# Weight tiles stored in memory as the chip holds them: one run of 16 KB per partition instead of eight of 2 KB

## The chip, the core and the metric

The kernel runs on one core of a Trainium2 chip. TensorE (PE) multiplies matrices, VectorE (DVE) and ScalarE (ACT) do elementwise work and reductions, GpSimd (POOL) and SyncE (SP) here mostly issue transfers, and sixteen DMA engines, shared by all queues, carry the data between the chip's memory and the on-chip buffer of 128 partitions. The metric is the device time of one execution in microseconds (us), median of several runs.

## What is computed

Two transformer-like blocks in float32 over 256 tokens of width 1024, cut to what matters here:

```python
# first block
h = rms_norm(x, attn_norm_g)
q, k, v, qi, ki, wi, glu_in, gates = split(h @ w_in)
y_att  = dsa_attention(...) @ w_att_out        # top-64 keys of each query
y_conv = conformer_conv(glu_in, ...) @ w_conv_out
x = x + (g0 * y_att + g1 * y_conv) @ w_out
h2 = rms_norm(x, ffn_norm_g)
x = x + peer(h2, w_peer_q, sub_keys, peer_u, peer_v)   # 128 expert rows per token, gathered
x = x + sigmoid(rms_norm(x) @ w_ple_gate) * (p @ w_ple_proj)
# second block
mod = silu(c) @ ada_w + ada_b                  # six modulation vectors, also for the context
ctx states = scans of mixer_block(modulate(rms_norm(ctx)))
x = x + g1 * mixer_block(modulate(rms_norm(x)), ctx states) @ w_out
x = x + g2 * (silu(dwconv(h @ up_gate)) * (h @ up_value)) @ w_down
return rms_norm(x) * final_g
```

## The kernel before

All dense weights come in tiles, in one order fixed by `weight_tiles`: 54 of them, most 1024 rows by 512 columns (2048 KB), held on the chip as 128 partitions by 8 chunks of 512 numbers. Two slots of a ring (`weights`) take them in turn. `sp_weights` issues their loads on SP's queue (L482): tile i as soon as the PE work on tile i-2 is done (`tile_done`). In memory the weights are plain matrices, so that a partition's share of a tile is 8 runs of 2 KB; a tile `up` is two loads with runs of 1 KB, `kiwi` two with runs of some 270 B, `down` one with runs of 4 KB. SP's queue also carries x, the constants, `lora_up` and `ctx` (`sp_ctx`, ahead of the tile ctx_lora) and the output. `pe_tile` makes PE wait for a tile's landing; the matmuls of tiles are at L502, L512, L755, L760, L752, L1269, L2157 and L2454.

Other queues share the DMA engines. POOL first loads small tables (`rel_bias`, `onehot`; PE's first step, L791, needs them), then the modulation weights `in_ada_wT`: 48 loads of 512 KB in runs of 4 KB into four slots (L1119), each issued when DVE has used the load four before it. DVE uses one with each L1135 (from the 17th load on), and these steps are woven by hand between DVE's others: three before each of the products with conv_out and att_out (L1067, L1072, L1075), ten behind L1075, then L1087 (x plus the first half of mix_out), eight more, and L1091 (x plus the second half), on which the next norm and the expert queries (peer_q tiles) depend. The queries lead to DVE's selection, and the first selected quarter lets POOL start the gather: 256 indirect loads of 128 expert rows of 8 KB (L1475) into a ring of eight, used by DVE (L1490), ACT and PE (L1521). The second block's context work runs beside the gather. After the gather come the second block's projections, scans and feed-forward part.

Of the kernel before, what the change touches and what calls it, by code (L numbers as in the profile page):

```python
# [25 lines left out]
P = 128  # L26
# [3 lines left out]
DC = D // P  # L30
# [4 lines left out]
CC = CONV_CH // P  # L35
# [9 lines left out]
DFF = ((8 * D // 3 + 127) // 128) * 128  # L45
FC = DFF // P
# [14 lines left out]
WSLOTS = 2  # L61
# [19 lines left out]
def const_columns():  # L81

    widths = dict(ident=P, eps=1, gn_eps=1, flip=P, lower=CH, upper=CH, lower_eq=CH, upper_eq=CH, lower_neg=CH, upper_neg=CH, head_mean=P, head_mean2=2, conv_mean=P,
                  ident2=HD, hide=TB * T, reset=RC * T, iota=NCAND, ident_q=QP, quad=QUADS)
    at, out = 0, {}
    for name, n in widths.items():
        out[name] = (at, n)
        at += n
    return out, at  # L90
# [48 lines left out]
    return (np.arange(REL_BUCKETS)[:, None] == bucket[None]).astype(np.float32)  # L139

def weight_tiles(dram):

    order = []

    def tile(name, *parts, width=512):
        order.append((name, width, parts))

    def part(w, k0, kc, c0, n, at=0):  # L150
        return (w[k0 * P:(k0 + kc) * P, c0:c0 + n].rearrange("(k p) n -> p k n", p=P), kc, at, n)

    w = dram["w_in"]
    tile("glu_g", part(w, 0, DC, GLU0 + 512, 512))
    tile("glu_a", part(w, 0, DC, GLU0, 512))
    for name, c in (("q", Q0), ("k", K0), ("v", V0), ("qi", QI0)):
        tile(name, part(w, 0, DC, c, 512))
    tile("kiwi", part(w, 0, DC, KI0, 64), part(w, 0, DC, KI0, 72, 64), width=136)
    for i in range(4):
        tile(f"gate{i}", part(w, 0, DC, GATE0 + 512 * i, 512))  # L160
    for i in range(2):
        tile(f"conv_out{i}", part(dram["w_conv_out"], 0, CC, 512 * i, 512))
    for i in range(2):
        tile(f"att_out{i}", part(dram["w_att_out"], 0, CC, 512 * i, 512))
    for i in range(2):
        tile(f"mix_out{i}", part(dram["w_out"], 0, DC, 512 * i, 512))
    for i in range(4):
        tile(f"peer_q{i}", part(dram["w_peer_q"], 0, DC, 512 * i, 512))

    w = dram["w_in_2"]  # L170
    tile("ctx_k", part(w, 0, DC, K20, 512))
    tile("ctx_v", part(w, 0, DC, V20, 512))
    tile("ctx_lora", part(w, 0, DC, LORA0, 128), width=128)
    for i in range(2):
        tile(f"ple_proj{i}", part(dram["w_ple_proj"], 0, 2, 512 * i, 512))
    for i in range(2):
        tile(f"ple_gate{i}", part(dram["w_ple_gate"], 0, DC, 512 * i, 512))
    tile("x_k", part(w, 0, DC, K20, 512))
    tile("x_lora", part(w, 0, DC, LORA0, 256), width=256)
    for name, c in (("x_v", V20), ("x_r", R0), ("x_cc", CC0), ("x_cx", CX0), ("x_cb", CB0)):  # L180
        tile(name, part(w, 0, DC, c, 512))
    for i in range(2):
        tile(f"rw_out{i}", part(dram["w_out_2"], 0, DC, 512 * i, 512))
    for i in range(FC // 2):
        tile(f"up{i}", part(dram["ffn_w_up"], 0, DC, 256 * i, 256),
             part(dram["ffn_w_up"], 0, DC, DFF + 256 * i, 256, 256))
    for i in range(0, FC, 4):
        tile(f"down{i // 4}", part(dram["ffn_w_down"], i, min(4, FC - i), 0, 1024), width=1024)
    return order

def build(nc, dram, out_dram):
    SC, n_small = small_columns()
    KC, n_const = const_columns()
    tiles = weight_tiles(dram)
    tile_at = {name: i for i, (name, _, _) in enumerate(tiles)}

    with ExitStack() as ctx:
        sems = {}

        def S(name):
            if name not in sems:
                sems[name] = ctx.enter_context(nc.semaphore(name))
            return sems[name]
# [4 lines left out]
        def sb(name, shape, dt=F32):  # L209
            return whole(ctx.enter_context(nc.sbuf_tensor(name, shape, dt)), shape)  # L210
# [22 lines left out]
        ring = sb("weights", [P, WSLOTS, 4096])  # L233
# [225 lines left out]
        n_parts = [0, 0]  # L459
        landed_at = []  # L460
        for i, (_, _, parts) in enumerate(tiles):
            n_parts[i % WSLOTS] += len(parts)
            landed_at.append(16 * n_parts[i % WSLOTS])

        def sp_weights(sp):
            for i, (name, width, parts) in enumerate(tiles):
                if name == "rw_out0":
                    sv_ = Solve(sp, True)
                    for who in ("pe", "act", "dve"):
                        sv_.wait(who, 3, sv_.events[who][-1])  # L470
                if name == "ctx_lora":
                    sp_ctx(sp)
                if name == "ple_proj1":
                    sp_last_tokens(sp)
                if name == "ple_gate0":
                    sp.wait_ge(S("cdone"), 1)
                    sp.wait_ge(S("dots_ok"), TB * GROUPS)
                if i >= WSLOTS:
                    sp.wait_ge(S("tile_done"), i - WSLOTS + 1)
                for view, kc, at, n in parts:  # L480
                    dst = ring[:, i % WSLOTS, 0:kc * width].rearrange("p (k n) -> p k n", n=width)
                    sp.dma_start(dst[:, :, at:at + n], view).then_inc(S(f"landed{i % WSLOTS}"), 16)  # L482
                if i == 0:
                    sp.dma_start(const[:, CONST_HEAD:], dram["const"][:, CONST_HEAD:]).then_inc(S("const_rest"), 16)

        def pe_tile(pe, name, buffer=True):

            i = tile_at[name]
            _, width, parts = tiles[i]
            pe.wait_ge(S(f"landed{i % WSLOTS}"), landed_at[i])  # L490
            if buffer and i >= 2:
                pe.wait_ge(S(f"freed{i % 2}"), i // 2)
            kc = parts[0][1]
            return ring[:, i % WSLOTS, 0:kc * width].rearrange("p (k n) -> p k n", n=width), G[i % 2]

        def pe_features(pe, name, act, n_chunks=4):

            w, out = pe_tile(pe, name)
            kc = w.shape[1]
            for c in range(n_chunks):  # L500
                for k in range(kc):
                    mm = nc.tensor.matmul(out[:, c * T:(c + 1) * T], w[:, k, c * P:(c + 1) * P], act[:, k, :],  # L502
                                          start=(k == 0), stop=(k == kc - 1))
            mm.then_inc(S("tile_done"), 1)

        def pe_tokens(pe, name, act):

            w, out = pe_tile(pe, name)
            kc = w.shape[1]
            for b in range(TB):  # L510
                for k in range(kc):
                    mm = nc.tensor.matmul(out[:, b * 512:(b + 1) * 512], act[:, k, b * P:(b + 1) * P], w[:, k, :],  # L512
                                          start=(k == 0), stop=(k == kc - 1))
                if b == 0 and name in HALF_TILES:
                    mm.then_inc(S("half_done"), 1)
            mm.then_inc(S("tile_done"), 1)
# [689 lines left out]
        def sp_last_tokens(sp):  # L1206
            sp.wait_ge(S("normed_out"), 16)
            sp.dma_start(quad_last, normed_rows[P:2 * P]).then_inc(S("last_tokens"), 16)
# [441 lines left out]
        def sp_ctx(sp):  # L1650
            wait_freed(sp, "mix_out1")
            act_load(sp, "lora", loraup, dram["lora_up"].rearrange("d p n -> p d n"))
            sp.wait_ge(S("sc_pe"), QUARTERS * TB)
            act_load(sp, "ctx", ctok, dram["ctx"].rearrange("(b p) d -> p b d", p=P))
# [1068 lines left out]
        @block.sync  # L2723
        def _(sp):
            sp_start(sp)
            sp_weights(sp)
            sp_end(sp)
# [85 lines left out]
```

## Time and profile before

| | |
|---|---|
| median of 3 runs | 1560.54 us (1558.47 to 1561.19) |
| span of the profiled execution | 1554.9 us |
| PE busy | 1212.9 us (78%) |
| DVE busy | 926.5 us (60%) |
| ACT / POOL busy | 431.5 us / 347.1 us |
| DMA | 409.73 MB in 109720 packets, mean 264 GB/s |
| of it SP's queue (q1) | 106.48 MB in 63552 packets, 19.2% of 16 engines |
| of it POOL's queue (q0) | 297.35 MB in 44576 packets, 46.5% |

A busy share is a mean over stages that have different limits; the stages have to be read one by one. The profiled execution's own time is its span of 1554.9 us; the runs' median lies 5.6 us above it.

### The profile page before, as it was taken

What the parts mean: (1) busy time and instruction counts of PE and PEld (TensorE: products, weight loads), DVE (VectorE), ACT (ScalarE), POOL (GpSimd) and SP (SyncE); (2) the same over time, 40 slices, a digit from 0 to 9 for tenths busy, and PEclk for the clock granted to TensorE, in tenths of its full rate; (3) what the DMA queues carried; (4) which work ended last, traced back from release to release, by engine and by line L of the source; (5) the groups of instructions that cost most, each with busy time, mean ns of one, the idle gap of its engine ahead of it and who ended that gap; (6) DMA issues with size and microseconds to landing.
All of it is one profiled execution on the core that took longest, in us unless ns stands there. A gap on an engine that the chain in (4) does not pass through costs nothing.

```text
span 1554.9 us, 26679 instructions
## 1 busy us (share of the span) xinstructions
PE 1212.9 (78%) x11282; PEld 834.9 (54%) x11282; DVE 926.5 (60%) x2067; ACT 431.5 (28%) x1094; POOL 347.1 (22%) x315
## 2 busy tenths in 40 slices
PE   7989898894385533457856775799987888999998
PEld 6467784772153100125524452468877774888843
DVE  2887666657797988785677655321455343455512
ACT  2111420132432422543364332423243211110100
POOL 1000012034354555454455544000000000000000
PEclk9997999996597855569878996899999999999999
DMA  9551459699999999999999999624300023344432
GB/s 381 195 191 66 144 205 390 238 383 419 414 410 420 420 422 421 421 414 419 416 421 420 420 418 418 240 82 163 109 9 3 4 111 108 122 163 161 137 140 104
DMA packets 109720, 409.73 MB, mean 264 GB/s; under 512 B 8456, under 2 KB 33552, under 8 KB 76448
## 3 DMA queue, kind: packets, MB, share of 16 engines
q0 software_dynamic: 44576, 297.35, 46.5%
q1 hardware_dynamic: 63552, 106.48, 19.2%
q10 hardware_dynamic: 1472, 4.20, 1.0%
q8 instruction: 88, 1.44, 0.4%
q14 instruction: 32, 0.26, 0.0%
HBM read 405.89 MB, written 2.11 MB: 262 GB/s over the span
## 4 chain that ended last, share of the span: by engine, by line
PE 58%; DMA 22%; DVE 10%; ACT 4%; issue 3%; POOL 2%; another core or an unknown queue 0%; POOLq 0%; DVEq 0%; ACTq 0%; SPq 0%
PE psum L502 20%; DMA arena<-in_experts,arena 17%; PE psum L1942 8%; PE psum L2454 5%; PE psum L512 4%; DVE arena L1490 4%; PE psum L1521 3%; DMA arena<-in_lora_up 2%; PE psum L755 2%; PE psum L1269 2%; POOL arena L1475 2%; PE psum L2244 2%; PE psum L760 2%; DMA arena<-in_ada_wT 2%; PE psum L741 2%
## 5 line engine op out<-in xcount | busy, mean ns | idle before, releaser
L1475 POOL DMA_INDIRECT arena<-in_experts,arena x256 | 317.1, 1239 | 383.2 <-PE psum L1521 299.8
L1521 PE MATMUL psum<-arena 128*32 128x512 f32 x1024 | 185.4, 805 | 238.2 <-ACT arena L1506 231.6
L502 PE MATMUL psum<-actT,weights 128*128 128x256 f32 x1312 | 287.3, 381 | 0.0
L502 PEld LDWEIGHTS psum<-actT,weights 128*128 128x128 f32 x1312 | 250.3, 191 | 35.7 <-issue 1.5
L1521 PEld LDWEIGHTS psum<-arena 128*32 128x32 f32 x1024 | 22.7, 121 | 329.5 <-ACT arena L1506 307.3
L1490 DVE CUSTOM_DVE_ANT_0 arena<-arena 128x1024 f32<-128x1024 f32 x96 | 116.7, 1224 | 50.9 <-DMA arena<-in_experts,arena 50.1
L1490 DVE CUSTOM_DVE_ANT_0 arena<-weights,arena 128x1024 f32<-128x1024 f32 x96 | 116.6, 1223 | 37.1 <-DMA arena<-in_experts,arena 35.1
L1496 ACT ACTIVATE arena<-arena 128x2 f32<-128x2 f32 x128 | 26.1, 204 | 364.3 <-DVE arena L1490 350.4
L1942 PE MATMUL psum<-arena 64*64 64x64 f32 (+1 forms) x2816 | 89.7, 231 | 17.4 <-DVE arena L2059 7.1
L1942 PEld LDWEIGHTS psum<-arena 64*64 64x64 f32 x2816 | 84.1, 142 | 26.0 <-issue 14.6
L1490 DVE CUSTOM_DVE_ANT_0 arena<-normed,arena 128x1024 f32<-128x1024 f32 x64 | 77.2, 1225 | 22.1 <-DMA arena<-in_experts,arena 20.3
L1119 POOL DMA_DIRECT2D arena<-in_ada_wT x48 | 25.5, 531 | 229.7 <-DVE mod L1135 229.7
L2454 PE MATMUL psum<-weights,arena 128*128 128x512 f32 x176 | 75.7, 592 | 0.0
L512 PE MATMUL psum<-weights,actT 128*128 128x512 f32 x160 | 69.2, 592 | 0.0
L1506 ACT ACTIVATE arena<-const,arena 128x32 f32<-128x32 f32 x256 | 66.3, 306 | 0.0
L1501 ACT ACTIVATE arena<-arena 128x1 f32<-128x1 f32 x256 | 61.5, 287 | 12.1 <-ACT arena L1496 0.4
L2528 DVE SCALAR_TENSOR_TENSOR arena<-arena,small 128x256 f32<-128x256 f32 x154 | 61.9, 478 | 0.0
L2454 PEld LDWEIGHTS psum<-weights,arena 128*128 128x128 f32 x176 | 33.4, 190 | 41.7 <-issue 41.6
L1942 PEld LDWEIGHTS psum<-actT,arena 64*64 64x64 f32 x1152 | 39.3, 134 | 21.4 <-ACT arena L2027 12.0
L512 PEld LDWEIGHTS psum<-weights,actT 128*128 128x128 f32 x160 | 30.4, 190 | 37.8 <-issue 37.8
L1942 PE MATMUL psum<-actT,arena 64*64 64x64 f32 x1152 | 45.5, 221 | 5.7 <-issue 4.3
L675 ACT ACTIVATE normed<-xres 128x512 f32<-128x512 f32 (+1 forms) x13 | 9.0, 692 | 146.4 <-DVE xres L2544 60.3
(390 smaller groups left out, 1897.0 us busy)
## 6 DMA issues: line engine op xcount, KB each, us to landing
weights<-in_w_in SPq DMA_DIRECT2D x18, 2048.0 KB
arena<-in_ada_wT POOLq DMA_DIRECT2D x48, 512.0 KB, 6.3
weights<-in_ffn_w_up SPq DMA_DIRECT2D x22, 1024.0 KB
weights<-in_ffn_w_down SPq DMA_DIRECT2D x5, 2048.0 KB
weights<-in_w_out SPq DMA_DIRECT2D x4, 2048.0 KB
weights<-in_w_peer_q SPq DMA_DIRECT2D x4, 2048.0 KB
arena<-in_experts,arena POOLq DMA_INDIRECT x256
weights<-in_w_ple_gate SPq DMA_DIRECT2D x2, 2048.0 KB
```

What stands on the lines that cost most here:

```text
L502: mm = nc.tensor.matmul(out[:, c * T:(c + 1) * T], w[:, k, c * P:(c + 1) * P], act[:, k, :], start=(k == 0), stop=(k == kc - 1))
L512: mm = nc.tensor.matmul(out[:, b * 512:(b + 1) * 512], act[:, k, b * P:(b + 1) * P], w[:, k, :], start=(k == 0), stop=(k == kc - 1))
L741: mm = nc.tensor.matmul(chunk_bank(c)[:, b * P:(b + 1) * P], xres[:, b, c * P:(c + 1) * P], norm_diag[:, b, :], start=True, stop=True)
L755: mm = nc.tensor.matmul(out[:, 2 * i * T:(2 * i + 1) * T], w[:, k, 2 * i * P:(2 * i + 1) * P], actT[:, k, :], start=(k == 0), stop=(k == D ...
L1475: nc.gpsimd.indirect_dma_start(out=rows[:, n % RING, :], out_offset=None, in_=dram["experts"], in_offset=bass.IndirectOffsetOnAxis(ap=eidx ...
L1490: ins = nc.vector.tensor_tensor_reduce(rows[:, pos, 0:D], quad_row(b, k % QUADS), rows[:, pos, 0:D], 1.0, 0.0, ALU.mult, ALU.add, dots[:, ...
L1501: nc.scalar.activation(acts[:, g, j:j + 1], gelu[:, g, j:j + 1], ACT.Copy, scale=gate[:, b, bass.ds(t * RING + (g * GROUP + j), 1)]).then_ ...
L1506: nc.scalar.activation(diag[:, pos, :], K("ident_q"), ACT.Copy, scale=acts[:, g, j:j + 1]).then_inc(S("diag_ok"), 1)
L1521: mm = nc.tensor.matmul(SUMS[sum_part(k, i), i, :], diag[:, pos, :], rows[:, pos, D + 512 * i:D + 512 * (i + 1)], start=first, stop=last, ...
L1942: mm = nc.tensor.matmul(dst[half[c], g, at + q * n:at + (q + 1) * n], left(g, c, q), right(g, c, q), start=True, stop=True)
L2454: return nc.tensor.matmul(aux[2 * b + n], ffT[:, f, b * P:(b + 1) * P], w[:, k, 512 * n:512 * (n + 1)], start=(f == 0), stop=(f == FC - 1))
L2528: st.run(nc.vector.scalar_tensor_tensor(dst, src, w, dst, ALU.mult, ALU.add))
```

## The change

Each weight tile is laid out beforehand as its own array of 128 rows, one row for each partition, in the order in which the chip holds it. A load is then one run for each partition: 16 KB for a full tile. `up` and `kiwi` become one load instead of two, and the counts that PE waits for follow (one landing for each tile). Tiles, order, slots, waits and arithmetic stay. Two tiles with the same contents (ctx_k and x_k, for one) share an array.

```diff
-    def part(w, k0, kc, c0, n, at=0):
-        return (w[k0 * P:(k0 + kc) * P, c0:c0 + n].rearrange("(k p) n -> p k n", p=P), kc, at, n)
+    def part(key, k0, kc, c0, n, at=0):
+        return key, k0, kc, c0, n, at
...
+def tile_sources():
+    first = {}
+    for name, _, parts in weight_tiles():
+        first.setdefault(parts, "tile_" + name)
+    return first
+
+def tile_arrays(arrays):
+    out = {}
+    for parts, name in tile_sources().items():
+        cuts = [arrays[key][k0 * P:(k0 + kc) * P, c0:c0 + n].reshape(kc, P, n) for key, k0, kc, c0, n, at in parts]
+        out[name] = np.ascontiguousarray(np.concatenate(cuts, axis=2).transpose(1, 0, 2)).reshape(P, -1)
+    return out
...
-            n_parts[i % WSLOTS] += len(parts)
+            n_parts[i % WSLOTS] += 1
...
-                for view, kc, at, n in parts:
-                    dst = ring[:, i % WSLOTS, 0:kc * width].rearrange("p (k n) -> p k n", n=width)
-                    sp.dma_start(dst[:, :, at:at + n], view).then_inc(S(f"landed{i % WSLOTS}"), 16)
+                kc = parts[0][2]
+                sp.dma_start(ring[:, i % WSLOTS, 0:kc * width], dram[sources[parts]]).then_inc(S(f"landed{i % WSLOTS}"), 16)
```

## Rows read from the trace of the kernel before

**Rows 1.** The page's second section: DMA busy tenths and rate in 40 slices.

```profile
DMA  9551459699999999999999999624300023344432
GB/s 381 195 191 66 144 205 390 238 383 419 414 410 420 420 422 421 421 414 419 416 421 420 420 418 418 240 82 163 109 9 3 4 111 108 122 163 161 137 140 104
```

**Rows 2.** Stretches: busy of PE, PEld, DVE, ACT, POOL (instructions); granted clock, DMA share, GB/s.

```profile
258.00:263.00 5.00, 5.00 (x14) 2.13 (x13) 3.95 (x7) 1.63 (x5) 1.27 (x3) 1.00 0.95 303
263.00:272.00 9.00, 8.74 (x21) 3.61 (x19) 4.93 (x8) 0.00 (x0) 1.92 (x4) 1.00 1.03 414
...
276.00:280.00 4.00, 1.72 (x8) 1.72 (x9) 2.46 (x8) 1.75 (x5) 0.53 (x1) 0.50 1.03 415
...
318.00:984.00 666.00, 408.51 (x4640) 216.53 (x4638) 491.21 (x1194) 253.42 (x793) 317.15 (x256) 0.76 1.01 418
...
420.00:440.00 20.00, 14.11 (x85) 8.10 (x85) 19.62 (x56) 6.41 (x23) 9.14 (x8) 0.83 0.97 393
...
1334.00:1472.00 138.00, 138.00 (x641) 121.49 (x640) 76.36 (x190) 16.87 (x41) 0.00 (x0) 1.00 0.45 153
```

**Rows 3.** POOL's waits, 300 to 985 us: us in total, times, longest.

```profile
POOL arena L1475 <- DVE arena L1444: 41.6, 1, 41.6
```

**Rows 4.** Timeline of DVE: start, us, operation [idle before, releaser].

```profile
240.00 1.23 DVE L1075 TENSOR_TENSOR arena<-arena 128x1024 f32<-128x1024 f32 x1
...
255.84 1.23 DVE L1135 CUSTOM_DVE_ANT_0 arena<-arena 128x1024 f32<-128x1024 f32 x1
257.11 1.23 DVE L1135 CUSTOM_DVE_ANT_0 arena<-arena 128x1024 f32<-128x1024 f32 x1
258.26 1.22 DVE L1087 TENSOR_TENSOR xres<-psum,xres 128x1024 f32<-128x1024 f32 x1
...
268.66 1.23 DVE L1135 CUSTOM_DVE_ANT_0 arena<-arena 128x1024 f32<-128x1024 f32 x1 [0.76 <-DMA arena<-in_ada_wT]
...
274.55 1.22 DVE L1135 CUSTOM_DVE_ANT_0 arena<-arena 128x1024 f32<-128x1024 f32 x1 [0.72 <-DMA arena<-in_ada_wT]
275.70 1.28 DVE L1091 TENSOR_TENSOR xres<-psum,xres 128x512 f32<-128x512 f32 x2
```

**Rows 5.** Timeline of PE around mix_out and at two norms.

```profile
242.34 2.44 PE L512 MATMUL psum<-weights,arena 128*128 128x512 f32 x4 [3.70 <-issue]
...
261.71 10.03 PE L512 MATMUL psum<-weights,arena 128*128 128x512 f32 x23
278.28 2.95 PE L741 MATMUL psum<-normed,xres 128*128 128x128 f32 x12 [6.54 <-DVE normed L722]
...
1316.62 1.83 PE L741 MATMUL psum<-normed,xres 128*128 128x128 f32 x12 [2.64 <-DVE normed L722]
```

**Rows 6.** Timeline of SP's queue: when a weight tile is issued.

```profile
231.14 0.37 SPq L482 DMA_DIRECT2D weights<-in_w_out  x1
238.67 0.37 SPq L482 DMA_DIRECT2D weights<-in_w_out  x1
258.04 0.37 SPq L482 DMA_DIRECT2D weights<-in_w_peer_q  x1
271.77 0.37 SPq L482 DMA_DIRECT2D weights<-in_w_peer_q  x1
...
356.53 0.37 SPq L482 DMA_DIRECT2D weights<-in_w_in  x1
```

**Rows 7.** The chain that ended last, in order of time: start, us, what.

```profile
356.95 32.78 DMA arena<-in_lora_up
...
389.81 11.80 DMA arena<-in_ctx
```

**Rows 8.** DMA issues: line, count, KB each, median us to landing.

```profile
xres<-in_x SPq DMA_DIRECT2D x1, 1024.0 KB, 5.1
...
bias_rows<-arena POOLq DMA_DIRECT2D x1, 12.0 KB, 4.8
```

**Rows 9.** The same chain at the start.

```profile
1.97 5.07 DMA arena<-in_onehot
```

More of the change, by code:

```diff
@@ L139, in bucket_onehot, with weight_tiles @@
     return (np.arange(REL_BUCKETS)[:, None] == bucket[None]).astype(np.float32)
-def weight_tiles(dram):
+def weight_tiles():
     order = []
@@ L148, in tile @@
         order.append((name, width, parts))
-    def part(w, k0, kc, c0, n, at=0):
-        return (w[k0 * P:(k0 + kc) * P, c0:c0 + n].rearrange("(k p) n -> p k n", p=P), kc, at, n)
-    w = dram["w_in"]
+    def part(key, k0, kc, c0, n, at=0):
+        return key, k0, kc, c0, n, at
+    w = "w_in"
     tile("glu_g", part(w, 0, DC, GLU0 + 512, 512))
@@ L161, in weight_tiles @@
     for i in range(2):
-        tile(f"conv_out{i}", part(dram["w_conv_out"], 0, CC, 512 * i, 512))
+        tile(f"conv_out{i}", part("w_conv_out", 0, CC, 512 * i, 512))
     for i in range(2):
-        tile(f"att_out{i}", part(dram["w_att_out"], 0, CC, 512 * i, 512))
+        tile(f"att_out{i}", part("w_att_out", 0, CC, 512 * i, 512))
     for i in range(2):
-        tile(f"mix_out{i}", part(dram["w_out"], 0, DC, 512 * i, 512))
+        tile(f"mix_out{i}", part("w_out", 0, DC, 512 * i, 512))
     for i in range(4):
-        tile(f"peer_q{i}", part(dram["w_peer_q"], 0, DC, 512 * i, 512))
-    w = dram["w_in_2"]
+        tile(f"peer_q{i}", part("w_peer_q", 0, DC, 512 * i, 512))
+    w = "w_in_2"
     tile("ctx_k", part(w, 0, DC, K20, 512))
@@ L174, in weight_tiles @@
     for i in range(2):
-        tile(f"ple_proj{i}", part(dram["w_ple_proj"], 0, 2, 512 * i, 512))
+        tile(f"ple_proj{i}", part("w_ple_proj", 0, 2, 512 * i, 512))
     for i in range(2):
-        tile(f"ple_gate{i}", part(dram["w_ple_gate"], 0, DC, 512 * i, 512))
+        tile(f"ple_gate{i}", part("w_ple_gate", 0, DC, 512 * i, 512))
     tile("x_k", part(w, 0, DC, K20, 512))
@@ L182, in weight_tiles @@
     for i in range(2):
-        tile(f"rw_out{i}", part(dram["w_out_2"], 0, DC, 512 * i, 512))
+        tile(f"rw_out{i}", part("w_out_2", 0, DC, 512 * i, 512))
     for i in range(FC // 2):
-        tile(f"up{i}", part(dram["ffn_w_up"], 0, DC, 256 * i, 256),
-             part(dram["ffn_w_up"], 0, DC, DFF + 256 * i, 256, 256))
+        tile(f"up{i}", part("ffn_w_up", 0, DC, 256 * i, 256),
+             part("ffn_w_up", 0, DC, DFF + 256 * i, 256, 256))
     for i in range(0, FC, 4):
-        tile(f"down{i // 4}", part(dram["ffn_w_down"], i, min(4, FC - i), 0, 1024), width=1024)
+        tile(f"down{i // 4}", part("ffn_w_down", i, min(4, FC - i), 0, 1024), width=1024)
     return order
+def tile_sources():
[9 more added lines that the diff above has]
+    return out
 def build(nc, dram, out_dram):
@@ L194, in build @@
     KC, n_const = const_columns()
-    tiles = weight_tiles(dram)
+    tiles, sources = weight_tiles(), tile_sources()
     tile_at = {name: i for i, (name, _, _) in enumerate(tiles)}
@@ L492, in pe_tile @@
                 pe.wait_ge(S(f"freed{i % 2}"), i // 2)
-            kc = parts[0][1]
+            kc = parts[0][2]
             return ring[:, i % WSLOTS, 0:kc * width].rearrange("p (k n) -> p k n", n=width), G[i % 2]
@@ L2801 @@
         "final_g": a["final_g_2"],
-        "w_in": a["w_in"][0], "w_conv_out": a["w_conv_out"][0], "w_att_out": a["w_att_out"][0],
-        "w_out": a["w_out"][0], "w_peer_q": a["w_peer_q"][0], "ada_wT": np.ascontiguousarray(a["ada_w_2"][0].T),
-        "w_in_2": a["w_in_2"][0], "w_ple_gate": a["w_ple_gate"][0], "w_ple_proj": a["w_ple_proj"][0],
-        "w_out_2": a["w_out_2"][0], "ffn_w_up": a["ffn_w_up_2"][0], "ffn_w_down": a["ffn_w_down_2"][0],
+        "ada_wT": np.ascontiguousarray(a["ada_w_2"][0].T),
+        **tile_arrays({
+            "w_in": a["w_in"][0], "w_conv_out": a["w_conv_out"][0], "w_att_out": a["w_att_out"][0],
+            "w_out": a["w_out"][0], "w_peer_q": a["w_peer_q"][0], "w_in_2": a["w_in_2"][0],
+            "w_ple_gate": a["w_ple_gate"][0], "w_ple_proj": a["w_ple_proj"][0], "w_out_2": a["w_out_2"][0],
+            "ffn_w_up": a["ffn_w_up_2"][0], "ffn_w_down": a["ffn_w_down_2"][0],
+        }),
     }
```

## The prediction

> **What bounds the kernel now.** I read the page's forty slices first: of 38.9 us each: the DMA engines are full in the first, in the seventh (233 to 272 us) and from the ninth to the twenty-fifth (the gather); elsewhere they have room [rows 1]. That splits the weight tiles, which all travel on SP's queue, into three kinds. (a) Tiles loaded beside a busy PE. From 1334 to 1472 us PE is busy 138.00 of 138.00 us while DMA stands at 0.45 [rows 2]; there a faster load is worth nothing, because each 2048 KB tile (2.10 MB) has 13.8 us of PE work in front of it. The same goes for the slices around 1014 to 1130 us, at 82 to 163 GB/s [rows 1]. (b) Tiles loaded during the gather of expert rows, which moves 418 GB/s over 666 us [rows 2]; its end is set by bytes, and the change moves the same bytes. The gather's first instruction waits 41.6 us for DVE's first selection [rows 3], so whatever delays that selection delays everything behind it. (c) Tiles loaded between 224 and 283 us, beside the stream of modulation weights (`in_ada_wT`, 48 loads of 512 KB, four slots, POOL's queue). Here is the place that counts: in the timeline of DVE each L1135 waits for a load, and L1091, which adds the last half of mix_out, stands behind the last of them and starts at 275.70 [rows 4]. PE had finished mix_out1 at 271.74 and sits idle until 278.28 [rows 5]. So about 4 us of the path are DMA, not PE.
>
> **Who gets the DMA.** lora_up (0.52 MB) was issued behind ctx_v (2.10 MB, issued at 356.53) on SP's queue [rows 6] and took 32.78 us [rows 7]: 2.62 MB in 32.8 us is 80 GB/s, 0.19 of 418. Both have 2 KB runs, the expert rows beside them 8 KB: 2/(2+8) is 0.20. The ctx load behind them (1.05 MB, 4 KB runs) took 11.80 us [rows 7]; without 2.6 us for start and finish (the xres load: 5.1 us for 1.05 MB, of which 2.5 is bytes at 414 GB/s [rows 8]) that is 114 GB/s, 0.27, against 4/12 = 0.33. And while peer_q0 loads in 2 KB runs, the last L1135 come 1.96 us apart (268.66 to 274.55, three steps) [rows 4]: 0.524 MB / 1.96 us is 267 of 414 GB/s [rows 2], 0.65, against 4/(4+2) = 0.67. So each DMA engine seems to give each queue one run in turn, and a queue's share goes by the length of its runs. With 16 KB runs the weights would take 16/20 = 0.80 beside ada_wT (332 GB/s, and 83 are left) and 16/24 = 0.67 beside the experts. The bytes stay; who is served first changes.
>
> The Trainium skill, "DMA: Bandwidth & Descriptors", section "Queues, rings and completion order", says that a DMA engine goes round the queues packet by packet, and a packet there holds some 9 to 17 descriptors. The trace agrees on the turns, but its 0.19 fits turns of one run. If a turn held so many runs of either queue, the shares would be the same.
>
> **Term A, the stretch from 231 to 276 us.** mix_out0 is issued at 231.14 [rows 6]; landing at 231.14 + 2.6 + 2.10/0.332 = 240.1. PE starts on it at 242.34 [rows 5], though DVE's last product ended at 241.23 [rows 4]: with the tile there, PE starts at 241.3, 1.0 us earlier. mix_out1 (issued 238.67) lands by 247.6, peer_q0 (issued 257) by 266. In each of these three windows of 6.3 us ada_wT gets 0.52 MB, one load where it now gets three. It loses four loads before L1087 and makes them up alone: alone, L1135 come 1.27 us apart (255.84 to 257.11 [rows 4]). Ten L1135 stand between L1075 and L1087. Two find their loads there (241.3 and 242.5), the third waits until about 247.0, seven more at 1.26 end at 257.1; L1087 starts at 257.1 instead of 258.26. Eight more follow: two at 258.4 and 259.6, the third inside the peer_q0 load at about 263.5, five more from 265.4 at 1.27 apart; the last ends at 271.8, against 275.77. PE, 1.0 us earlier, ends mix_out1 at 270.7, so L1091 starts at 271.8: A = -4.0. From 258 to 263 the trace moves only 303 GB/s where 414 follow [rows 2], a loss of 1.3 us; with 16 KB runs waiting I expect that hole closed, and -4.0 contains this. Bounds: -4.5 (PE's end decides) and +3 (below, second rival). I take -3.5, near the hand schedule, since the four slots may not restart without a gap.
>
> **Term B, PE's clock after that wait.** After 6.54 us idle the twelve L741 records take 2.95 us; in the later stage with the same code, after 2.64 us idle, 1.83 [rows 5]. The granted clock was 0.50 from 276 to 280 us [rows 2], the 1.2 GHz level. With a gap of 2.6 to 3 us some of the 1.1 us goes: B = -0.5, bounds -1.1 and 0.
>
> **Term C, the gather.** It starts earlier by A + B and lasts as long, since it is bytes. peer_q3 lands about when the gather begins. ctx_v needs about 2.6 + 2.10/0.28 = 10 us instead of most of 32.8, lora_up and ctx follow some 17 us earlier, and DVE, which now waits for ctx, no longer crowds the work behind it: from 420 to 440 us DVE is busy 19.62 of 20 and the DMA rate falls to 393 [rows 2], a loss of 25 GB/s for 20 us, 1.2 us. I take half: C = -0.6, bounds -1.2 and +0.5 (if the bursts of 67% open such a hole elsewhere).
>
> **Term D, the start.** PE's first step waits for onehot, 48 KB on POOL's queue, issued at 1.97, 5.07 us [rows 9]. Its last runs meet glu_g on SP's queue, and with 16 KB runs a turn is eight times longer: 16 KB at 414/16 GB/s is 0.63 us instead of 0.08. The nearest row is the bias_rows store, 4.8 us [rows 8], which ran beside the 9.6 KB runs of const: no slower. So 0 by that row, at most two turns, 1.3 us; D = +0.4.
>
> **Term E, fewer instructions.** kiwi and eleven up tiles need one DMA instead of two: 12 issues of 0.37 us on SP's queue [rows 6], all where SP waits for PE. Cost nothing, gain nothing; if SP were late the tile would still have its 13.8 us. PE waits on the same tiles; no wait is added, and nothing new stands behind one.
>
> **Sum.** -3.5 - 0.5 - 0.6 + 0.4 = -4.2 us on the profiled 1554.9 us of span. The median of the runs, 1560.54, lies 5.6 us above that span, which I carry over: 1556.3.
>
> **Rivals.** First (the forecast, 0.53): 1556.3, its own range 1554 to 1558.5. Second, slower (0.19): the last L1135 must have its load before peer_q1, issued when PE ends mix_out1 at 270.7, brings its first bytes about 1.5 us later, at 272.2. My schedule has that load landed at 270.5, 1.7 us ahead. If stalls of the four slots eat this margin, the load meets a queue that takes 0.80, and what is left of 0.52 MB goes at 83 GB/s, up to 6.3 us instead of 1.3: L1091 at 277 to 279 instead of 275.7. A is then about +2, B 0, C -0.6, D +0.4: 1562.3. For it speaks that ada_wT has only four slots; against it that the loads make 1.27 us each when alone. No load here has them; at half the rate the 7.6 MB of weights inside the gather (peer_q3, ctx_k, ctx_v, ctx_lora, ple_proj) would cost 18 us: 1578.
>
> By the section "Specifications" of the same page of the Trainium skill, runs of 512 B or more already go at line rate. By that rule the length of a run gains nothing in itself, which is the third rival's time, 1560.5, with its chance; the trace agrees as far as 2 KB runs beside 4 KB ones move 414 GB/s.
>
> **How the numbers follow.** About 0.2% (3.1 us) is what a measurement here can tell from no change. The forecast's own spread puts 0.43 below 1557.4 and 0.10 above it; with the third rival within 0.2% is 0.33; second and fourth give slower 0.24. The range 1554 to 1563.5 leaves out some 0.07 below, the fourth rival and the upper part of the second.
>
> **What would show it.** Right: lora_up lands after some 15 us instead of 32.78; PE starts mix_out0 near 241.3; L1135 shows two long waits (some 3 to 4 us) in place of seven short ones; L1091 near 272; the first gather near 314.5; and the rest shifted as one piece. Wrong: lora_up unchanged (third rival), a wait of over 3 us right before L1091 (second), tiles of 2.10 MB that take over 8 us when alone (fourth), onehot landing after 8 us (D too small).

## The result

The changed kernel takes 1565.22 us (median of 6 runs, 1563.46 to 1567.41); the kernel before, run beside it, 1559.84 us (6 runs, 1557.52 to 1561.59). The ratio is 1.0034, 95% interval 1.0023 to 1.0046: slower by some 5.4 us, where 4.2 us faster was forecast. The same kernel measured again gave 1.0043 (e11, below). The profiled span is 1561.4 us against 1554.9.

First the changes in traffic that were meant. From the page of the changed kernel, the DMA part of the slices and the count of packets:

```profile
GB/s 386 193 189 67 137 222 376 207 349 420 420 422 421 415 422 422 420 419 417 419 420 419 420 418 413 254 81 162 108 9 3 4 111 108 122 162 160 135 143 101
DMA packets 55767, 409.72 MB, mean 262 GB/s; under 512 B 6216, under 2 KB 6736, under 8 KB 16096
```

Half the packets (before: 109720), the same bytes. In the seventh and the eighth slice (233 to 311 us) the rate is lower than before: 376 and 207 instead of 390 and 238 [rows 1].

Now the place that counts. The timeline of DVE in the changed kernel (start, us, operation, [idle before, releaser]); all line numbers have grown by 16, so that L1151 is the former L1135, L1103 the former L1087 and L1107 the former L1091:

```profile
245.39 1.23 DVE L1151 CUSTOM_DVE_ANT_0 arena<-arena 128x1024 f32<-128x1024 f32 x1 [1.89 <-DMA arena<-in_ada_wT]
249.10 1.23 DVE L1151 CUSTOM_DVE_ANT_0 arena<-arena 128x1024 f32<-128x1024 f32 x1 [2.48 <-DMA arena<-in_ada_wT]
...
259.62 1.22 DVE L1103 TENSOR_TENSOR xres<-psum,xres 128x1024 f32<-128x1024 f32 x1
264.07 1.23 DVE L1151 CUSTOM_DVE_ANT_0 arena<-arena 128x1024 f32<-128x1024 f32 x1 [3.23 <-DMA arena<-in_ada_wT]
...
271.99 1.23 DVE L1151 CUSTOM_DVE_ANT_0 arena<-arena 128x1024 f32<-128x1024 f32 x1 [0.41 <-DMA arena<-in_ada_wT]
279.60 1.23 DVE L1151 CUSTOM_DVE_ANT_0 arena<-arena 128x1024 f32<-128x1024 f32 x1 [6.37 <-DMA arena<-in_ada_wT]
280.75 1.22 DVE L1151 CUSTOM_DVE_ANT_0 arena<-arena 128x1024 f32<-128x1024 f32 x1
281.89 1.29 DVE L1107 TENSOR_TENSOR xres<-psum,xres 128x512 f32<-128x512 f32 x2
```

One wait of 6.37 us stands two steps ahead of L1107, which starts at 281.89 instead of 275.70 [rows 4]: +6.2 us. DVE's waits for these loads from 231 to 285 us (us in total, times, longest), in the kernel before and below it in the kernel after, differ by as much:

```profile
DVE arena L1135 <- DMA arena<-in_ada_wT: 11.2, 12, 2.2
```

```profile
DVE arena L1151 <- DMA arena<-in_ada_wT: 17.5, 9, 6.4
```

The load that DVE waits for is the last link of the DMA kind on the chain that ended last in this stretch (start, us, what); the first line is one from the stretch's beginning, for comparison:

```profile
242.65 7.71 DMA arena<-in_ada_wT
...
268.74 10.83 DMA arena<-in_ada_wT
```

The two weight tiles beside it, from the timeline of SP's queue (start of the first, time from there to the end of the second, count):

```profile
255.18 14.06 SPq L498 DMA_DIRECT2D weights<-in_tile_peer_q  x2
```

peer_q0 is issued at 255.18 and peer_q1 at about 268.9, that is 0.2 us after the slow load of 512 KB; before, they went at 258.04 and 271.77 [rows 6]. Why they go earlier is on the timeline of PE:

```profile
241.14 27.73 PE L528 MATMUL psum<-weights,arena 128*128 128x512 f32 x64 [2.65 <-DVE arena L1091]
284.47 0.80 PE L757 MATMUL psum<-normed,xres 128*128 128x128 f32 x2 [15.60 <-DVE normed L738]
```

mix_out starts 1.2 us earlier (242.34 before) and its 64 matmuls take 27.73 us instead of 29.40, so PE is done at 268.87 instead of 271.74 [rows 5], and then idles 15.60 us instead of 6.54. Everything behind is moved as one piece, as POOL's first gather and its wait show:

```profile
324.54 1.01 POOL L1491 DMA_INDIRECT arena<-in_experts,arena  x1 [41.74 <-DVE arena L1460]
```

It stands 6.28 us later than before (318.26), its wait for the selection as long as it was (41.6 [rows 3]).

Cut into stages by the first instructions of each, the profiles read (us; "to L1107" is from mix_out0's issue to the second add; "to gather" from there to the first gather; "gather" up to the issue of ple_gate0; "rest" to the end of the span):

| kernel | span | to mix_out0 | to L1107 | to gather | gather | rest |
|---|---|---|---|---|---|---|
| before | 1554.9 | 231.14 | 44.56 | 42.56 | 670.28 | 566.4 |
| after | 1561.4 | 230.92 | 50.97 | 42.65 | 669.60 | 567.3 |

Of +6.5 us, +6.4 lie in one stage of 45 us, -0.7 in the gather, +0.9 in the rest, where PE's clock stood on another level at one norm (below, term B).

### The profile page after: what moved, and what is told of

Read it like the earlier page. It is cut to its first block, busy times and chain, and to the rows that moved or that the text cites. A ratio compares the mean times of both kernels' runs of the same rounds, so it can differ in the third digit from the quotient of the medians.

```text
span 1561.4 us, 26667 instructions
## 1 busy us (share of the span) xinstructions
PE 1208.4 (77%) x11282; PEld 828.9 (53%) x11282; DVE 927.6 (59%) x2067; ACT 430.3 (28%) x1094; POOL 350.1 (22%) x315
## 3 DMA queue, kind: packets, MB, share of 16 engines
q0 software_dynamic: 44576, 297.35, 46.5%
## 4 chain that ended last, share of the span: by engine, by line
PE 54%; DMA 27%; DVE 9%; ACT 4%; issue 3%; POOL 2%; POOLq 0%; DVEq 0%; ACTq 0%
DMA arena<-in_experts,arena 23%; PE psum L518 19%; PE psum L1958 5%; PE psum L2470 5%; PE psum L528 4%; DVE arena L1506 3%; PE psum L1537 3%; POOL arena L1491 2%; DMA arena<-in_ada_wT 2%; PE psum L771 2%; PE psum L2260 2%; PE psum L776 2%; PE psum L1285 2%; PE psum L757 2%; PE psum L768 1%
## 5 line engine op out<-in xcount | busy, mean ns | idle before, releaser
L1537 PE MATMUL psum<-arena 128*32 128x512 f32 x1024 | 189.4, 820 | 249.2 <-ACT arena L1522 249.0
L1958 PE MATMUL psum<-arena 64*64 64x64 f32 (+1 forms) x2816 | 82.4, 226 | 15.4 <-DVE arena L2075 7.1
L1958 PEld LDWEIGHTS psum<-arena 64*64 64x64 f32 x2816 | 78.5, 139 | 23.6 <-issue 12.2
L1135 POOL DMA_DIRECT2D arena<-in_ada_wT x48 | 25.3, 528 | 236.1 <-DVE mod L1151 236.1
L2470 PEld LDWEIGHTS psum<-weights,arena 128*128 128x128 f32 x176 | 33.4, 190 | 41.7 <-issue 41.6
L757 PE MATMUL psum<-normed,xres 128*128 128x128 f32 x160 | 29.4, 329 | 26.5 <-DVE normed L738 21.5
```

Source lines behind the costliest of these rows:

```text
L757: mm = nc.tensor.matmul(chunk_bank(c)[:, b * P:(b + 1) * P], xres[:, b, c * P:(c + 1) * P], norm_diag[:, b, :], start=True, stop=True)
L1537: mm = nc.tensor.matmul(SUMS[sum_part(k, i), i, :], diag[:, pos, :], rows[:, pos, D + 512 * i:D + 512 * (i + 1)], start=first, stop=last, ...
L1958: mm = nc.tensor.matmul(dst[half[c], g, at + q * n:at + (q + 1) * n], left(g, c, q), right(g, c, q), start=True, stop=True)
L2470: return nc.tensor.matmul(aux[2 * b + n], ffT[:, f, b * P:(b + 1) * P], w[:, k, 512 * n:512 * (n + 1)], start=(f == 0), stop=(f == FC - 1))
```

## The experiments

The theory after the result: a DMA engine gives the queues turns of equally many runs, so that weight tiles in 16 KB runs take most of the traffic beside the 4 KB runs of `in_ada_wT`; the modulation loads between mix_out0 and L1107 come late, and one of the last meets peer_q1. The main rival: tiles in an order of their own are slower to load or cost PE time, wherever they are. All ratios are to the kernel before, run beside each batch, with 95% intervals.

**Length of the runs alone (e1, e12, e8).** The tiles stay arrays of their own, but in blocks, so that a partition's share comes in eight runs of 2 KB (e1) or four of 4 KB (e12, and e8, the same kernel run once for its profile):

```diff
-                sp.dma_start(ring[:, i % WSLOTS, 0:kc * width], dram[sources[parts]]).then_inc(...)
+                r = runs_of(sources[parts][5:], kc)        # e1: kc; e8, e12: max(kc // 2, 1)
+                dst = ring[:, i % WSLOTS, 0:kc * width].rearrange("p (r m) -> p r m", r=r)
+                sp.dma_start(dst, dram[sources[parts]].rearrange("(r p) m -> p r m", p=P)).then_inc(...)
```

> Each tile still lies in memory by itself, as in the changed kernel, but cut into eight blocks of 128 rows, so that a partition gets eight runs of 2 KB as in the kernel before; one load for each tile. Theory (turns: a DMA engine takes one run of each queue in turn, and 16 KB runs of the peer_q tiles crowd out the modulation weights): as the kernel before, ratio 0.998 to 1.002, lora_up lands after 31 to 34 us, the add of mix_out's second half starts at 275 to 276.5 us. Rival (place: where the tile lies in memory or its regular step is what costs): as the changed kernel, ratio 1.003, lora_up as in the changed kernel (17 us), the add near 282 us.

> All tiles cut into blocks so that a partition gets four runs of 4 KB (two rows of 2 KB joined). Only one look, for the share of a queue by its run length. Theory (turns): beside 8 KB expert rows the weights get 4/12; lora_up, behind ctx_v, lands after 22 to 26 us (32.8 at 2 KB, 17.3 at 16 KB). Rival (share by queue, not by run): 31 us or more, or 18 or less as with 16 KB.

> e8 (four runs of 4 KB for each partition), now timed: the weights and the modulation weights, whose runs are 4 KB too, share evenly. Theory: no load waits over 3 us before the add, 44 to 46 us after mix_out0 is issued; the gather keeps about half of its 0.6 us; ratio 0.998 to 1.001. Rival (tile order costs by itself, as in e1): ratio 1.002 to 1.005.

e1: 1564.63 us, 1.0040 (1.0024 to 1.0056). e12: 1560.52 us, 1.0015 (0.9999 to 1.0031). e8: one run of 1556.17 us. e12's ratio lies between what was expected of the theory (up to 1.001) and of the rival (from 1.002). The stage to L1107 is 44.8 us in e1, 44.8 in e12 and 45.1 in e8: with short runs the long wait is gone. The load of lora_up behind ctx_v, which measures a queue's share beside the gather, follows the run. From the DMA issues (last column: median us to landing) of e8, and below it of the kernel after:

```profile
arena<-in_lora_up SPq DMA_DIRECT2D x1, 512.0 KB, 24.1
```

```profile
arena<-in_lora_up SPq DMA_DIRECT2D x1, 512.0 KB, 17.2
```

32.8 us with 2 KB [rows 7] (34.6 in e15), 24.1 with 4 KB, 17.2 with 16 KB. With the prediction's shares (ctx_v's run over itself plus 8 KB, 2/10 for lora_up behind it, 418 GB/s) and its 2.6 us for start and finish, an estimate gives some 34, 24 and 16. So a queue's share follows the length of its runs, and "shares don't follow the run" (third rival) is out. The Trainium skill, "DMA: Bandwidth & Descriptors", section "Queues, rings and completion order", has a DMA engine go round its queues by packets of some 9 to 17 descriptors. The three times don't speak against that: turns of equally many runs give the same shares as turns of one run, so these times can't tell one from the other.

But e1's total is not that of the kernel before, which was expected. Its profile has +1.5 us ahead of mix_out0 (no evidence, since this stage lies between 230.6 and 232.8 us in all profiles) and +3.3 from the fourth norm to x_cc, where PE waits 0.47 us for x_v and then runs 64 matmuls in 15.77 us instead of 14.06. That cost is taken up again with e16.

**Which of the peer_q tiles (e2, e3, e5).** e2 is e1 with peer_q1 alone in 16 KB runs (`r = 1 if name == "peer_q1" else kc`), e3 the changed kernel with peer_q0 and peer_q1 in blocks of 2 KB runs (`r = kc if name in ("peer_q0", "peer_q1") else 1`). e5 is the kernel before with peer_q1 alone as an array in 16 KB runs; all others come from their matrices:

```diff
+                if name in LONG:                            # LONG = ("peer_q1",)
+                    sp.dma_start(ring[:, i % WSLOTS, 0:kc * width], dram[tile_key(name)]).then_inc(...)
+                else:
                     for key, k0, kc, c0, n, at in parts:
```

> All tiles as in e1 (eight runs of 2 KB) but peer_q1, which has one run of 16 KB. Theory (turns): PE ends mix_out1 at about 271.7 and peer_q1 goes out; the last load of modulation weights that the add needs is then half landed and gets a fifth of the engines, so one wait of 3 to 6 us (now 0.7) stands before the add, which starts at 278 to 281 us; ratio 1.0015 to 1.0035. Rival (it takes all the tiles, or peer_q0's load is what costs): ratio within 0.999 to 1.001, the add at 275 to 276.5 us.

> All tiles with one run for each partition, but peer_q0 and peer_q1 with eight of 2 KB. Theory (turns): the mix_out tiles still land early, PE ends mix_out1 at 269 us as in the changed kernel, the long wait before the add is gone, the add starts at 272 to 276 us, the gather keeps its 0.6 us: ratio 0.997 to 1.000. Rival (late landing of all tiles, or their place, is what costs): ratio 1.002 to 1.0035, the add after 279 us.

> The kernel before, every tile read from its matrix as it was, but peer_q1 alone laid out with one run of 16 KB for each partition (e1 has shown that 2 KB runs in the tile's own order are themselves slower, so that e2 had no clean base). Theory (turns): one wait of 3 to 7 us in front of the add of mix_out's second half instead of 0.7; the add starts 48 to 50.5 us after mix_out0 is issued (44.6 in the kernel before); ratio 1.002 to 1.004. Rival (the loss needs long runs in all tiles, or is in the later stages): 44 to 46 us, ratio 0.999 to 1.001.

e2: 1564.34 us, 1.0025 (1.0006 to 1.0045), stage to L1107 50.2 us, with one wait of 4.86 us before the last step: peer_q1's long runs bring a wait back into e1's profile. On the time e2 is no slower than e1 (1.0040), and its profile is of the slowest of its seven runs (1569.35 us), so the wait's price is not shown by this pair. e3: 1560.18 us, 1.0014 (1.0000 to 1.0028), 45.7 us: without the two tiles' long runs the wait is gone, but the expected 0.997 to 1.000 was missed. e5: 1557.96 us, 0.9995 (0.9979 to 1.0011), 44.6 us: here the expected wait of 3 to 7 us did not come. Its timeline of DVE ends ahead of the add with

```profile
274.09 1.22 DVE L1155 CUSTOM_DVE_ANT_0 arena<-arena 128x1024 f32<-128x1024 f32 x1 [0.62 <-DMA arena<-in_ada_wT]
```

and PE in e5 ended mix_out1 only at 272.2 (242.81 + 29.40), so that peer_q1, issued at 272.24, found the last modulation load nearly landed. So peer_q1's long runs alone did no harm here, where they started behind these loads. That speaks for a race, which the changed kernel loses from both sides: PE is earlier and the loads are later. e2 fits in: its loads came in 2 KB runs as in e5, but PE's 64 matmuls took 27.70 us and not 29.40, so that peer_q1 went out 1.7 us sooner after mix_out's start.

**The four tiles of the stretch (e6, e14).** The changed kernel, but mix_out0, mix_out1, peer_q0 and peer_q1 come from their matrices in 2 KB runs (`LONG` = all names but these four); e14 is the same kernel once more.

> The changed kernel, but the four tiles that load beside the modulation weights (mix_out0, mix_out1, peer_q0, peer_q1) are read from their matrices in 2 KB runs as in the kernel before. Theory (turns): the whole loss is gone; the add starts 44 to 46 us after mix_out0 is issued, the gather lasts 0.6 us less; ratio 0.998 to 1.0005. Rival (part of the loss is in other tiles or later stages): ratio 1.002 or more.

> The kernel of e6_after_but_mix_peer once more, unchanged: the changed kernel with mix_out0, mix_out1, peer_q0 and peer_q1 read from their matrices in runs of 2 KB. If the whole loss lies in the stretch from mix_out0 to L1091: L1091 at 42.5 to 45 us after the issue of mix_out0 and the ratio to the kernel before 0.998 to 1.000, as at first (42.9 us, 0.9992). If the layout of the other tiles loses something elsewhere: above 1.001.

e6: 1556.66 us, 0.9992 (0.9977 to 1.0007); e14: 1558.88 us, 0.9995 (0.9982 to 1.0008). Stage to L1107 42.9 and 45.1 us. In e6 the last steps of DVE run without a wait:

```profile
270.80 1.22 DVE L1155 CUSTOM_DVE_ANT_0 arena<-arena 128x1024 f32<-128x1024 f32 x1 [0.81 <-DMA arena<-in_ada_wT]
271.95 1.22 DVE L1155 CUSTOM_DVE_ANT_0 arena<-arena 128x1024 f32<-128x1024 f32 x1
273.18 1.22 DVE L1155 CUSTOM_DVE_ANT_0 arena<-arena 128x1024 f32<-128x1024 f32 x1
274.33 1.28 DVE L1111 TENSOR_TENSOR xres<-psum,xres 128x512 f32<-128x512 f32 x2
```

So the loss goes with four tiles of 54, and the other fifty in 16 KB runs cost nothing that can be measured (the intervals end at 1.0007 and 1.0008), and gain nothing. That also answers the main rival for 16 KB runs; e4 and e10 below answer it from the other side, since there every tile keeps its order and runs and only the time of issue changes. A version that beats the kernel before by more than its interval was not found.

**peer_q1 alone undone (e9, e13).** The changed kernel with peer_q1 alone from its matrix; e13 is the same kernel again.

> The changed kernel with peer_q1 alone read from its matrix in 2 KB runs. e5 showed no loss from a 16 KB peer_q1 alone, since the last load of modulation weights had landed before its first bytes. Theory (a race: the early mix_out0 and the late modulation weights let peer_q1 come in front of the last two loads, and its 16 KB runs then keep them waiting): the 6 us wait shrinks to 1 to 2.5 us, the add starts 44.5 to 47 us after mix_out0 is issued, ratio to the kernel before 0.9985 to 1.0015. Rival (peer_q0's long runs are the loss, peer_q1 only shows it): 49 us or more, ratio 1.002 to 1.004.

> The kernel of e9_after_peer_q1_2k once more, unchanged: the changed kernel with peer_q1 alone read from its matrix in runs of 2 KB. In its first profile L1091 still came 49.5 us after the issue of mix_out0 (four single waits of 0.7 to 2.2 us in place of one of 6.4), yet its time was 0.35% below that of the changed kernel. If peer_q1's long runs alone make the loss: the ratio again 1.000 to 1.002, and L1091 mostly before 47 us. If the three other tiles do their part, as that profile says: L1091 again near 49.5 us and the ratio 1.001 to 1.003. If that timing was luck: 1.003 or more.

e9: 1560.99 us, 1.0008 (0.9996 to 1.0020); e13: 1563.63 us, 1.0026 (1.0012 to 1.0040). The stage to L1107 took 49.5 and 49.1 us, where 44.5 to 47 was expected. DVE in e13:

```profile
260.45 1.22 DVE L1107 TENSOR_TENSOR xres<-psum,xres 128x1024 f32<-128x1024 f32 x1
261.59 1.21 DVE L1155 CUSTOM_DVE_ANT_0 arena<-arena 128x1024 f32<-128x1024 f32 x1
267.65 1.23 DVE L1155 CUSTOM_DVE_ANT_0 arena<-arena 128x1024 f32<-128x1024 f32 x1 [4.84 <-DMA arena<-in_ada_wT]
...
278.06 1.22 DVE L1155 CUSTOM_DVE_ANT_0 arena<-arena 128x1024 f32<-128x1024 f32 x1 [2.83 <-DMA arena<-in_ada_wT]
280.06 1.23 DVE L1155 CUSTOM_DVE_ANT_0 arena<-arena 128x1024 f32<-128x1024 f32 x1 [0.76 <-DMA arena<-in_ada_wT]
281.21 1.28 DVE L1111 TENSOR_TENSOR xres<-psum,xres 128x512 f32<-128x512 f32 x2
```

The wait during peer_q1 is shorter (2.83 for 6.37), but the one during peer_q0 is there (4.84), and the loads behind it come that much later. My first reading, that peer_q1 alone makes the loss, was too narrow: by these profiles peer_q0's long runs make the loads late, and peer_q1's then add to it. How much of the loss is each tile's share these two timings leave open between 1.0008 and 1.0026.

**Holding the tiles back (e4, e10, e7).** SP waits until DVE has used so many modulation loads before it issues a peer_q tile. e4 is the changed kernel with both held, e10 with peer_q1 alone, e7 the kernel before with peer_q0 held until 42 and, as 16 KB runs, only the tiles loaded inside the gather (peer_q3, ctx_k, ctx_v, ctx_lora, ple_proj):

```diff
+                for held, used in (("peer_q0", 41), ("peer_q1", 44)):      # e10: peer_q1 alone
+                    if name == held:
+                        sp.wait_ge(S("ada_used"), used)
```

> The changed kernel, with two waits on SP's queue: peer_q0 goes out when 41 of the 48 loads of modulation weights are used, peer_q1 when 44 are (those that stand before the add). Theory (turns): with no other load beside them the last eight uses come about 1.3 us apart, the add starts at 268.5 to 272 us, PE may then wait up to 2 us for peer_q0; ratio 0.995 to 0.998. Rival (the loss is in the tiles themselves): ratio 1.001 to 1.004, and later peer_q tiles make it worse.

> The changed kernel with one wait on SP's queue: peer_q1 goes out when 44 loads of modulation weights are used, that is with the add. Theory (race): the last two loads come without a neighbour, 1.3 to 1.8 us apart, the add starts 44 to 46.5 us after mix_out0 is issued, peer_q1 still lands 10 us before PE needs it; ratio 0.998 to 1.001. Rival (peer_q0's long runs): 48 us or more, ratio 1.0015 or more.

> The kernel before with 16 KB runs only for tiles that load beside the gather (peer_q3, ctx_k, ctx_v, ctx_lora, ple_proj), and with a wait on SP's queue: peer_q0 goes out when 42 of 48 loads of modulation weights are used. Theory (turns): the eight uses behind the first add come about 1.3 us apart, the second add starts 40.5 to 42 us after mix_out0 is issued (PE's end of mix_out1 then decides), peer_q0 lands just in time (0 to 1 us of wait), the gather lasts 0.6 us less: ratio 0.9965 to 0.999. Rival (the modulation stream is bound by its four slots and its queue, not by sharing): 44 to 45 us, ratio 0.999 to 1.002.

e4: 1559.62 us, 1.0007 (0.9991 to 1.0023), stage to L1107 41.75 us, the next one 46.3. e10: 1560.1 us, 1.0005 (0.9989 to 1.0020), 47.5 us. e7: 1561.19 us, 1.0021 (1.0004 to 1.0038), 41.0 us, the next one 50.4. The gains expected of e4 and e7 (up to 0.998 and 0.999) did not come. With the tiles out of the way the second add comes 3 us earlier than before, which is what the change hoped for, but then PE waits for the tile that was held, 0.57 us in e4 and 5.02 in e7, and works behind it at a granted clock of 0.50 (e4, 280 to 286 us; 0.90 in the kernel before). PE in e7:

```profile
275.11 2.95 PE L763 MATMUL psum<-normed,xres 128*128 128x128 f32 x12 [2.95 <-DVE normed L744]
283.08 2.08 PE L777 MATMUL psum<-actT,weights 128*128 128x256 f32 x4 [5.02 <-DMA weights<-in_w_peer_q]
```

So these orders of issue got no 4 us out of the stretch: the loads of both queues are needed at its end, and who is served first decided who waits. A hold that ends earlier was not tried. e10 shows on the time what peer_q1's place is worth (1.0005 against 1.0043 in the same batch), by a way that leaves the run length alone. Its profile, of one of its slowest runs (1562.96 us), missed the expected 44 to 46.5 us: a wait of 5.58 us stands in it beside peer_q0's long runs.

**The changed kernel and the kernel before again (e11, e15).** No edits.

> The changed kernel as it is, once more beside the next three, so that they have it on the same chip. Expected: ratio 1.002 to 1.005, one wait of 5 to 7 us before the add of mix_out's second half, which starts 50 to 52 us after mix_out0 is issued.

> The kernel before, once more, for the spread of one kernel's stages between two profiles. If differences of 1 to 2 us between profiles in stages that no edit touches (from the start to mix_out0 230.6 to 232.8 us, from the fourth norm to x_cc 59.3 to 62.1, from there to the fifth norm 222.4 to 225.7) are the chip's own: such a stage of this profile differs from the first one (231.1, 60.9, 224.6) by 1 us or more while L1091 stays at 44 to 46 us after mix_out0. If they belong to the kernels: all within 0.5 us of the first profile. Ratio 0.998 to 1.002.

e11: 1564.8 us, 1.0043 (1.0023 to 1.0062), stage to L1107 50.9 us, with one wait of 7.39 us ahead of the last two steps: the wait stands in both profiles of the changed kernel. e15: 1558.54 us, 0.9995 (0.9983 to 1.0007), stage to L1107 44.7 us. But other stages, which no edit touches, differ between the two profiles of the kernel before: from the add to the gather 42.56 and 44.13, from the fourth norm to x_cc 60.91 and 59.45 us. Differences of 1 to 1.6 us there are no evidence for a kernel. The stage to L1107 varies too: in five profiles of kernels that read its four tiles alike, from the matrices (before, e15, e6, e14 and e16), it took 42.9 to 47.3 us. e10's 47.5 lies at the edge of that, the 50.9 and 51.0 of the changed kernel and the 49.1 to 50.2 of e13, e9 and e2 clearly outside.

**Where 2 KB runs in blocks lose (e16).** The kernel before with the block order of e1 from ctx_k on; the tiles up to peer_q3 come from their matrices.

> The kernel before, but the tiles from ctx_k on are arrays of their own in tile order, with eight runs of 2 KB for each partition, as in e1_runs2k; the tiles up to peer_q3 come from their matrices. e1 cost 0.4% without any long wait. If that cost is in the loads of the second block (x_v landing 0.5 us late, and a lower granted clock behind it): ratio 1.003 to 1.005, and PE waits some 0.5 us for x_v. If it is in the first 320 us: 0.999 to 1.001. A value between says both.

e16: 1561.33 us, 1.0023 (1.0008 to 1.0037), between the two answers. The 64 matmuls of x_v take 14.08 us and do not wait, so that e1's slow x_v was not the place. And the stage to L1107, where its edits do nothing, took 47.3 us in its profile, with PE's clock up in mix_out (27.70 us for the 64) and peer_q0 out at 256.2. So what e1 and e16 lose is not settled: the length of a run doesn't explain it, nor do the late tiles' loads by any wait that I found; where the arrays lie in memory was not tried.

**PE's clock at mix_out.** The 64 matmuls of mix_out take 27.70 to 27.73 us in six of the eighteen profiles (after, e11, e2, e6, e9, e16) and 29.20 to 30.27 in the other twelve. With 2.65 us of idle time ahead of them both occur: 27.73 in after, e11 and e9, and 29.20 to 29.27 in e3, e4, e10 and e13. With 3.48 us or more there are only long ones (before 3.70, e15 3.48, e5 4.54). The granted clock decides. Over the first 2 us of mix_out (columns as in [rows 2]), in the kernel after and below it in e13:

```profile
241.10:243.10 2.00, 1.96 (x5) 1.00 (x6) 1.98 (x3) 0.00 (x0) 0.45 (x1) 1.00 1.12 469
```

```profile
241.80:243.80 2.00, 2.00 (x3) 0.97 (x4) 2.00 (x3) 0.00 (x0) 0.51 (x1) 0.50 1.12 469
```

After the same 2.65 us idle it is 1.00 in one (2.4 GHz) and 0.50 in the other (1.2 GHz). That gives or takes 1.6 us of PE's end, and so of peer_q1's issue. Both profiles of the changed kernel have the upper level; what its wait would be at the lower one is not shown. The nearest pair is e9 and e13, with 49.5 us at the upper level and 49.1 at the lower.

## Why the prediction was wrong, point by point

**What bounds, and the shares: right.** The stretch from 231 to 276 us was the one that decided, and a queue's share followed its run: lora_up took 17.2 us, where some 15 was forecast, ctx_v's long runs ahead of it included.

**Term A: the step that failed.** It was to give -3.5 us and measured +6.2. The second rival had the mechanism (a late modulation load that meets peer_q1's long runs), the mark in the profile (a wait of over 3 us right before the add) and the size of the wait (up to 6.3; 6.37 measured). It was put at 0.19 because the hand schedule left the last load 1.7 us ahead of peer_q1's first bytes. That margin was made of three terms of the schedule, and all three were off:

- The catch-up. A wait up to 247.0 was to be followed by seven uses at 1.26 us each, with L1087 at 257.1. The third use came at 245.39 and the fourth, behind a second wait, at 249.10; three uses came at that pace, then waits of 0.99 and 0.83 us came back, and L1103 stood at 259.62. The pace of 1.27 was read from two neighbouring steps [rows 4] for which the loads had already landed. A longer row of steps without a tile beside them, in e7, has seven steps in 11.71 us (259.67 to 271.38; peer_q0 goes out at 269.01, near their end), 1.67 each: the four slots don't restart at once, since the next load of a slot is only issued when DVE has used the last. The hole at 258 to 263 us did close (423 GB/s), but another one opened before it: from 240 to 256 us the DMA engines moved 367 GB/s in the kernel after (379 in e11), 412 before (394 in e15).
- The tile beside the later loads. Of the eight uses behind L1087, two were to be done before peer_q0's bytes came in the way, and the third at about 263.5. peer_q0 went at 255.18, not 257, and it was the first of the eight that came at 264.07, behind a wait of 3.23 us: two loads behind the schedule.
- PE's end. It was carried over with its 29.40 us less 1.0, at 270.7. It was 268.87: 1.2 us from the earlier start, which was right (241.14 for 241.3), and 1.7 from the granted clock, which by chance had not fallen. The price of a clock step in mix_out was not in the sum.

Together the load was issued at 268.74 and peer_q1 at 268.9: no margin was left. The term's upper bound of +3 was also short: it took the add at 277 to 279, from a wait of 6.3 us on a schedule that ended early; on the schedule as it ran the same wait put the add at 281.89. The price of the wait was good, the chance was not: a margin of 1.7 us, worked out over eighteen uses of four slots, was no reason for 0.19.

The rival's own time was 1562.3; the kernel took 1565.2, and 1563.5 was the range's end. What it left out is some 2.9 us: a later add (281.89, not up to 279).

**Term B: wrong, nothing of the -0.5 came.** It counted on a shorter wait of PE and a clock that stays up. The wait got longer (15.60 us), and the twelve records behind it took 2.96 us (2.95 before). And the row that it took for a short wait's price is no price: at the fifth norm, after 2.64 us idle as before, the changed kernel's twelve records took 2.95 us where the kernel before took 1.83 [rows 5]:

```profile
1321.98 2.95 PE L757 MATMUL psum<-normed,xres 128*128 128x128 f32 x12 [2.64 <-DVE normed L738]
```

The stage from this norm to the first up tile is 1.2 us longer for it. The twelve records took 2.95 us in both profiles of the changed kernel and 1.83 in both of the kernel before; whether that is the change's doing is not shown (e9, e10 and e13 have 2.95; e6 and e14 have 1.83). That the length of the idle time alone doesn't tell on which level PE runs behind it, one kernel shows by itself: at the fourth norm, after 3.27 us idle each time, the twelve records took 2.42 us in the first profile of the kernel before and 1.83 in the second (e15).

**Term C: right.** -0.7 us (669.60 for 670.28), -0.6 forecast. The second profiles have 669.99 (e11) and 670.33 (e15), and the 50 tiles alone 669.38 and 669.42 (e6, e14). The hole at 420 to 440 us is closed:

```profile
420.00:440.00 20.00, 14.62 (x68) 7.87 (x68) 19.59 (x52) 8.13 (x25) 9.75 (x8) 0.64 1.01 422
```

422 GB/s instead of 393 [rows 2].

**Term D: the delay was right, its price was nothing.** The chain of the changed kernel begins with

```profile
1.97 5.43 DMA arena<-in_onehot
```

+0.36 us for +0.4 forecast [rows 9]; at 18 us the two kernels stand side by side again (the products of L771 at 17.76, those of L755 at 17.80 before).

**Term E: right.** Twelve issues fewer show in none of the stages.

**The fourth rival: its sign showed, its price did not.** The sign was a tile of 2.10 MB that takes over 8 us when alone. The five full tiles `down`, which load with nothing beside them, land after 8.5 us in the kernel after (median us in the last column; 7.9 in e11), and below it after 7.7 in the kernel before (e15):

```profile
weights<-in_tile_down SPq DMA_DIRECT2D x5, 2048.0 KB, 8.5
```

```profile
weights<-in_ffn_w_down SPq DMA_DIRECT2D x5, 2048.0 KB, 7.7
```

So a lone tile in 16 KB runs lands 0.2 to 0.8 us later than one in 4 KB runs. That is far from half the rate, it stands in front of 13.8 us of PE work, and the gather did not get longer (term C). The section "Specifications" of the same page of the Trainium skill, "DMA: Bandwidth & Descriptors", has transfers of 512 B or more at line rate. The trace agrees in that the longer run gave a lone tile nothing; it also took a little.

**The third rival** would have been nearest to the time of the fifty other tiles (e6: 0.9992, e14: 0.9995), though not for its reason: the shares did change (lora_up lands after 17.1 us in e6 too), but apart from the 0.7 us of the gather that moved nothing on the path.

## What to carry to other kernels

A change of layout that leaves the bytes alone still shifts who is served first: before giving one queue longer runs, look for a stream in shorter runs beside it that ends on the critical path, and leave the tiles beside it as they are. A margin of 1 or 2 us that comes out of a schedule made by hand is a coin to toss: take the pace from a long row of steps, not from two neighbours, and let the case behind the margin have half of the chance. And of PE's time after a wait, take the slower of the levels that the rows show as one end of the range, whatever the wait's length.

## What the runs showed of the hardware that was not expected

- When a weight tile had landed early, the modulation loads left behind in four slots of 512 KB did not fill the DMA engines: from 251 to 256 us the kernel after moved 251 GB/s (280 in e11), the kernel before 402 (347 in e15). In e7, with peer_q0 held, they moved 310 GB/s from 259.67 to 269 us.
- The granted clock behind a wait of 2.6 to 3.2 us was 0.50 in some profiles and 1.00 in others, at the same place of nearly the same kernels (mix_out 29.3 or 27.7 us; the fifth norm's records 2.95 or 1.83 us), and behind 3.27 us it differed between two profiles of one kernel (the fourth norm's records 2.42 or 1.83 us). What decides was not found.
- Tile arrays in blocks with 2 KB runs lost 0.2 to 0.4% (e1, e16) although the kernel before has runs of the same length; the cause is open.
